# Norms between the first feed-forward layer and the state space layer: squared planes folded on VectorE before TensorE's ones product

## The reference, cut to what matters

```python
def rms_norm(x, w):
    xf = x.astype(jnp.float32)
    y = xf * lax.rsqrt(jnp.mean(xf * xf, axis=-1, keepdims=True) + EPS)
    return (y * w.astype(jnp.float32)).astype(x.dtype)

for i in range(DEPTH):
    hn = rms_norm(h, norm_mix_pre[i])
    m = mixer(hn)                              # DeltaNet and attention (i = 0), S5 state space (i = 1)
    h = h + rms_norm(m, norm_mix_post[i])
    hn = rms_norm(h, norm_ffn_pre[i])
    f = swiglu_ffn(hn, ffn_w_gate[i], ffn_w_up[i], ffn_w_down[i])
    h = h + rms_norm(f, norm_ffn_post[i])
```

## Time and profile before

| | |
|---|---|
| device time, median of 3 runs | 2748.59 us (2748.31 to 2750.68) |
| span of the profiled execution | 2748.7 us, first to last instruction |
| PE busy | 2678.9 us (97%), 18073 matmuls |
| DVE busy | 1266.2 us (46%) |
| ACT busy | 626.3 us (23%) |
| POOL busy | 1015.0 us (37%) |
| mean granted TensorE clock | 0.992 |
| chain that ended last | PE 89%, DVE 6%, ACT 2%, issue 2%, DMA 1% |

### The profile page before, as it was taken

One profiled execution on the slowest core, in us unless ns is written; L12 is line 12 of the kernel. 1 busy time (PEld: TensorE's weight loads), 2 busy tenths in 40 slices (PEclk: granted clock), 3 DMA queues, 4 the chain that ended last, 5 costly groups with the idle time before them and its releaser, 6 DMA issues.

```text
span 2748.7 us, 44704 instructions
## 1 busy us (share of the span) xinstructions
PE 2678.9 (97%) x18073; PEld 2555.5 (93%) x18073; DVE 1266.2 (46%) x2119; ACT 626.3 (23%) x1108; POOL 1015.0 (37%) x462
## 2 busy tenths in 40 slices
PE   8999999999999999999999999899999999999998
PEld 7999788866999999999999989899899999999997
DVE  5666667566174444444442457612632222222235
ACT  4231333365151000000000342411420000000002
POOL 5444110034354444444333325052544444444440
PEclk9999999999999999999999999999999999999999
DMA  4236321110232222222223139641231111111112
GB/s 163 93 109 136 97 69 57 49 62 25 87 113 67 76 82 82 82 78 79 81 76 96 52 124 283 219 115 42 98 108 46 46 46 46 46 46 46 46 31 82
DMA packets 142550, 232.27 MB, mean 84 GB/s; under 512 B 34016, under 2 KB 104928, under 8 KB 140256
## 3 DMA queue, kind: packets, MB, share of 16 engines
q1 hardware_dynamic: 53552, 134.98, 15.9%
q10 hardware_dynamic: 88880, 95.59, 11.0%
HBM read 172.78 MB, written 61.96 MB: 85 GB/s over the span
## 4 chain that ended last, share of the span: by engine, by line
PE 89%; DVE 6%; ACT 2%; issue 2%; DMA 1%; POOL 0%; ACTq 0%; DVEq 0%; POOLq 0%
PE psum L806 25%; PE psum L807 24%; PE psum L808 24%; PE psum L892 2%; PE psum L1295 2%; PE psum L1269 1%; DVE area L2282 1%; DVE area L2249 1%; PE psum L1117 1%; DVE x_lo L2294 1%; PE psum L1282 1%; PE psum L1138 1%; PE psum L1387 1%; DMA resid<-area 1%; DVE area L2272 1%
## 5 line engine op out<-in xcount | busy, mean ns | idle before, releaser
L806 PE MATMUL psum<-x_hi,w_hi 128*128 128x344 f32 (+2 forms) x3456 | 1123.9, 325 | 0.7 <-issue 0.7
L807 PE MATMUL psum<-x_lo,w_hi 128*128 128x344 f32 (+2 forms) x3456 | 1105.5, 320 | 0.0
L808 PE MATMUL psum<-x_hi,w_lo 128*128 128x344 f32 (+2 forms) x3456 | 1104.9, 320 | 0.0
L764 POOL TENSOR_TENSOR w_hi<-stage,const 128x1024 fp32r<-128x1024 f32 x193 | 484.6, 2511 | 1515.0 <-PE psum L808 1346.5
L806 PEld LDWEIGHTS psum<-x_hi,w_hi 128*128 128x128 f32 x3456 | 650.0, 188 | 11.1 <-issue 3.7
L807 PEld LDWEIGHTS psum<-x_lo,w_hi 128*128 128x128 f32 x3456 | 650.0, 188 | 3.3 <-issue 1.7
L808 PEld LDWEIGHTS psum<-x_hi,w_lo 128*128 128x128 f32 x3456 | 649.4, 188 | 0.0
L767 POOL TENSOR_TENSOR w_lo<-stage,w_hi 128x1024 fp32r<-128x1024 f32 x193 | 486.3, 2520 | 15.1
L2754 DVE TENSOR_TENSOR area<-area,psum 128x344 f32<-128x344 f32 (+2 forms) x132 | 67.7, 513 | 653.4 <-ACT area L1971 653.4
L806 PE MATMUL psum<-act_hi,w_hi 128*128 128x344 f32 (+2 forms) x1056 | 341.6, 323 | 8.3 <-DVE area L2777 6.9
L808 PE MATMUL psum<-act_hi,w_lo 128*128 128x344 f32 (+2 forms) x1056 | 336.9, 319 | 0.0
(11 more groups left out here) (235 smaller groups left out, 2233.8 us busy)
## 6 DMA issues: line engine op xcount, KB each, us to landing
stage<-wstream SPq DMA_DIRECT2D x193, 512.0 KB, 3.5
s_set<-area ACTq DMA_DIRECT2D x8, 1600.0 KB, 7.1
proj<-area ACTq DMA_DIRECT2D x20, 520.0 KB, 2.7
area<-proj ACTq DMA_DIRECT2D x36, 256.0 KB, 3.7
resid<-area ACTq DMA_DIRECT2D x6, 1376.0 KB, 6.0
area<-resid ACTq DMA_DIRECT2D x6, 1376.0 KB, 11.4
area<-s SPq DMA_DIRECT2D x8, 1024.0 KB, 6.7
area<-proj ACTq DMA_DIRECT2D x12, 520.0 KB, 4.8
```

Source lines behind the costliest of these rows:

```text
L764: pool.tensor_tensor(per_block(w_hi[:, slot, :]), src, ones_block, ALU.mult).then_inc(high_split, 1)
L806: mm(out[:, 0:n], w_hi[:, slot, wk], hi[:, xk, a:a + n], start=first, stop=False)
L807: mm(out[:, 0:n], w_hi[:, slot, wk], lo[:, xk, a:a + n], start=False, stop=False)
L808: return mm(out[:, 0:n], w_lo[:, slot, wk], hi[:, xk, a:a + n], start=False, stop=last)
```

## The change

```diff
         def folded(r):
 
-            return r in (1, 3)
+            return r in (1, 2, 3)
 
         def fold_event(r, c, m):
 
-            return 6 * (r // 2) + 2 * c + m
+            return 6 * (r - 1) + 2 * c + m
...
                 add_down(end, 0)
+                if folded(r + 1):
+                    square_fold(r + 1, 0, 0)
                 step(end, 3)
                 norm_post(r + 1, 0)
                 step_product(end, 4)
                 add_down(end, 1, tiles=range(0, 2))
                 step_low(end, 4)
+                if folded(r + 1):
+                    square_fold(r + 1, 0, 1)
                 add_down(end, 1, tiles=range(2, KT))
...
                 norm_pre(r + 1, 0)
+                square_fold(r + 1, 1, 0)
                 step(end, 5)
...
             ffn(0, 1)
+            square_fold(2, 1, 1)
             norm_pre(2, 1)
             norm_low(2, 1)
+            square_fold(2, 2, 0)
             norm_post(2, 2)
+            square_fold(2, 2, 1)
             norm_pre(2, 2)
             norm_low(2, 2)
```

## The result

The changed kernel takes 2759.37 us (median of 4 runs, 2758.29 to 2763.79) beside 2748.45 for the kernel before in the same measurement (4 runs, 2747.31 to 2750.68). The ratio is 1.0042, with an interval of 1.0028 to 1.0056: slower, by 10.9 us between the medians. The forecast was 2759.4 and slower.

A forecast was written before the change was run, and what follows sets the result against it. TensorE was busy 2678.9 of 2748.7 us, but the last three sums already waited on their operand chain. Work -14.1, waits +17.9 and clock 2.4 + 2.4 + 2.2 gave +10.8 on 2748.6: 2759.4, range 2752.5 to 2764.

The forecast's parts named there:

- The work removed: At the six changed sums on TensorE: 2.35 us less for each, 14.1 us of work in all.
- fold(0,1) and the lock: At the second sum: GpSimd's split holds the shared ports, fold ends at 1564.3, TensorE idles 4.6 us at tile 5.
- The FFN's end: After the first three sums: waits on steps set by GpSimd's split take back the gain, leaving 0.0.
- The last three sums: At sum(1,1), sum(2,0), sum(2,1): TensorE idles 4.9, 6.8 and about 3.7 us, leaving 3.8 late.
- Waits and work together: Over the six sums: 14.1 us gained, 17.9 lost in waits, +3.8 us.
- The clock: Behind three new TensorE idle gaps: half clock adds 2.4, 2.4 and 2.2 us.
- the fourth gap: Idle stretch of about 3.7 us ahead of sum(2,1): nothing counted for the clock, upper bound 3.1.
- the first rival: The clock falls only in the longest gap, ahead of sum(2,0): +6.2 us, 2754.8; chance 0.17.
- Longest gap only: Half clock only behind the longest gap, ahead of sum(2,0): 3.8 + 2.4 = +6.2 us, 2754.8; chance 0.17.
- Cheap folds: fold(0,1) gets the ports before GpSimd's second split and the clock holds: +1.5 to +3.8 us, 2750.1 to 2752.4; chance 0.13.
- Every gap in full: All four idle gaps: waits plus clock cost in full, +15.5 us, 2764.1; chance 0.10.
- TensorE's work counts: Over the whole stretch, TensorE's saved work decides: faster by 14.1 us, 2734.5 in full; chance 0.05.

The follow-up runs named there:

- e6: Changed kernel with GpSimd's second split instruction made to wait until fold(0,1) is done; 2758.07 us, ratio 1.0039 to the kernel before.
- e4: Kernel before with only the first three folds, fold(0,1) placed behind the fifth add_down in VectorE's queue; 2746.01 us, ratio 0.9993 to the kernel before.
- e1: Kernel before with folds only at sum(0,0), sum(0,1) and sum(1,0); 2749.50 us, ratio 1.0005 to the kernel before.
- e3: Changed kernel with unread products run on TensorE in the four idle gaps; 2752.25 us, ratio 1.0018 to the kernel before.
- e2: Kernel before with folds only at sum(1,1), sum(2,0) and sum(2,1); 2759.17 us, ratio 1.0039 to the kernel before.
- e5: Changed kernel with fold(2,0) put ahead of the two x_lo instructions in VectorE's queue; 2757.86 us, ratio 1.0035 to the kernel before.
- e10: Kernel before, unchanged, run once more for another profile; 2748.23 us (one run).
- e9: Changed kernel, unaltered, run once more for another profile; 2761.82 us (one run).
- e8: Kernel before with only 11 unread products added on TensorE ahead of sum(1,1) of r = 3; 2748.41 us, ratio 1.0000 to the kernel before.

## Why the prediction was right

**The work removed.** Six sums at 2.35 us less. sum(0,0), sum(0,1) and sum(1,0) went to 2.48 to 2.53, as in the earlier trace rows. TensorE's busy time fell by 10.7. The sum 14.1 less 7.8 for the clock gives 6.3, and in the local stretch it fell by 6.1 (108.9 to 102.8); another 4.7 fell ahead of sum(0,0), where nothing is changed, and 0.2 came back behind the stretch.

**fold(0,1) and the lock.** Forecast: start at 1560.4, 4 us long, end 1564.3, third add_down done at 1564.8, TensorE idle 4.6. Measured, with 3.83 added: 1560.37, 3.87, 1564.24, and 4.46 idle. e6 confirmed the cause (1.63 once GpSimd waits) and e4 that the place in the queue turns it into a cost. The page of the Trainium skill that the prediction named (SBUF — State Buffer, "SBUF: two separate sides") holds: the fold was held for the rest of GpSimd's instruction. It held GpSimd as well: its next split, queued behind the second, started at 1558.89 and took 4.25 while the fold ran to 1560.41, where the same instruction took 2.94 in the earlier trace rows.

**The FFN's end.** Forecast: 0.0 left of the three shorter sums. e1, which has only these three, comes to -0.2 without its clock.

**The last three sums.** Idle 4.9, 6.8 and 3.7 were forecast; 4.99, 6.77 and 3.39 came. Waits of the three for L2272: 15.1 (forecast "some 15"). The 6.8 doesn't follow from the working, though: 1.74 of before, plus 5.4 late, less 0.6 late at the sum ahead, makes 6.5. With the clock held (e3) sum(2,0) started 5.7 late against sum(0,0), and that gives the 6.8. Nor is all of it the fold's own time: in the changed kernel the second square of sum(1,1) runs from 1598.01 to 1599.36 and its fold from 1599.39 to 1600.98, and no run tells the wait for the second squares from the fold.

**Waits and work together.** Forecast +3.8. The changed kernel and its repeat show +3.5 and +3.3, and e3, where the clock cannot count, +4.2. The first two have part of the clock taken back in a wait: the stretch ahead of sum(2,1) was 3.39 and 3.30 there, and 3.79 to 3.83 in e2, e5 and e6.

**The clock.** Forecast 7.0 in three terms, 2.2 + 2.4 + 2.4, and nothing for the fourth gap. Measured 7.8 in four, by half of the slow work: 1.5 at tile 5, 1.9 at sum(1,1), 2.9 at sum(2,0), 1.5 at sum(2,1); holding the clock (e3) took 7.1 off the local figure. That the total came out this close is luck: the first two gaps were cheaper than I had taken, by 0.7 and 0.5, sum(2,0) was dearer by 0.5, and the fourth gap, counted at nothing, cost 1.5. The reason behind it was weaker than it looked. I had placed the new gaps by their nearness to 1.89 ("clock held") and 5.52 ("clock fell"). The clock also fell behind 2.54 (e5), 2.21 (e6) and 1.88 (e10), so the row of 1.89 in the trace of before was one draw and no bound. For a gap of 1.9 us my reasoning would have counted nothing, and half of the profiles would have contradicted it. The Trainium skill (TensorE: Matmul & The Clock Gate, Part 1) says that the moment varies between runs of one kernel, and before and e10, one kernel at 1.00 and at 0.50 behind the same 1.88 to 1.89 us, bear that out.

The sentence under the first rival, that nothing shows a fall below 5.5 us, was wrong on the trace of before itself. These are its timeline and a window in layer 0, far from the change:

```profile
683.65 2.07 PE L1282 MATMUL psum<-const,area 128*128 128x128 f32 x9 [1.51 <-DVE area L2718]
...
684.00:685.00 1.00, 1.00 (x6) 1.00 (x5) 0.00 (x0) 0.32 (x1) 1.00 (x1) 0.50 0.00 0
```

Behind an idle stretch of 1.51 us, with one of 0.80 us that ended at 679.90, the clock was at 0.50 from 683.9 to 690.7; it fell there in 12 of the 13 profiles. So reading the clock over the whole trace, and not only at the longest gaps, would have told that gaps of 2 us and less can be followed by a fall.

**The rivals.** "Longest gap only" fell with the four low stretches. "Cheap folds" fell with fold(0,1) at 3.87. "Every gap in full" had the four right and the prices too high. "TensorE's work counts" is refuted by e2: three sums less work, 11.3 us slower.

**Left open.** Among kernels with all six folds and no unread products the slow work in the local stretch was 15.3 to 20.1 us, and I can't say what sets it: e5 had a shorter idle stretch ahead of sum(2,0) and more slow work. The local figures of e9 and the changed kernel agree within 0.3 us, but one profile of e5 doesn't tell whether its 20.1 is its own or a draw. The kernel before gave 113.94 and 115.12, so 11.24 is the difference to the luckier of its two profiles; to the other it is 10.1.

## What to carry to other kernels

Halving an instruction's work on the busiest engine counts only where its operand is there early; where the engine already waits for the operand, the instruction that halves it is added to the chain, so read the wait ahead of each instance, one by one, before summing. Price an added instruction by what stands behind it in its queue and what its ports collide with (the same fold cost 4.5 us of idle TensorE in one place and 0.8 three instructions later). Idle time on TensorE costs again through the clock, in this kernel behind stretches as short as 1.5 us, and a single profile that shows the clock holding is no bound on that.

## What I had not expected of the hardware

- The clock fell to 0.50 behind idle stretches of 1.88, 2.21 and 2.54 us, and behind the 1.88 only in three of six profiles. Far from the change it fell behind one of 1.51 us (near 680 us of the span) in 12 of 13 profiles, and behind one of 1.93 to 1.95 us (near 286 us) in 6 of 13.
- A low stretch cost 1.5 to 2.9 us in the changed kernel, by half of the slow work in it, and the length of it didn't follow the length of the gap: 3.4 us low behind 3.39 and 4.46 us of idle time, 10.2 behind 6.77, and in e5 6.8 behind the 4.47 that cost the changed kernel 3.4.
- Unread products (nine with 256 columns ran for 4.05 us in e3) kept the clock at 1.00 in all four gaps, and since they fill time in which TensorE waits anyway, they cost only what they overrun. Held clock is gained time only until the next wait, as e8 shows.
